# The scores of the attention's first two units in the program ahead of the barrier, and PSUM banks in another order

## What is computed

```python
def compress(kv, w1, w2, pe):          # blocks of 32 rows, stride 16
    pre = lo[:, :-1] + hi[:, 1:] + pe_term[:, None, :]
    return jnp.einsum('bnche,ced->bnchd', jax.nn.gelu(pre), w2)

def nsa_core(q, qpos, gates, cmp_kv, fetch, n_sel, win_kv, win_pos):
    # three branches: compressed, selected, window; each
    s = jnp.einsum('btkgd,bnkd->bkgtn', qg, keys) - slopes * d
    p = masked_softmax(s, mask)        # exp(s - max) / max(sum, 1e-30)
    o = jnp.einsum('bkgtn,bnkd->btkgd', p, values)
    # o = g[0] * o_cmp + g[1] * o_slc + g[2] * o_win
```

## Time and profile before

| | |
|---|---|
| median of 3 runs | 1879.27 us (1876.8 to 1881.36) |
| the profiled execution | 1880.03 us, its span 1878.3 us |
| TensorE busy | 1832.9 us (98%) |
| VectorE, ScalarE, GpSimd busy | 49%, 35%, 33% |
| front, up to its barrier | 0 to 544.8 us |
| clearing of semaphores, second barrier | 544.9 to 546.1 us |
| attention's first TensorE instruction | 546.24 us |
| attention's first transpose of weights | 553.18 us |
| output projection starts | 897.5 us |

### The profile page before, as it was taken

The page is one execution under the profiler, slowest core; times in us unless marked ns, Lnnn a source line. Parts: engine busy times, 40 slices in busy tenths (PEclk is TensorE's granted clock), DMA queues, the critical chain, the costliest instruction groups (busy, mean ns, idle before and its releaser), DMA issues.

```text
span 1878.3 us, 34536 instructions
## 1 busy us (share of the span) xinstructions
PE 1832.9 (98%) x13412; PEld 1715.7 (91%) x13412; DVE 915.4 (49%) x1624; ACT 662.9 (35%) x1247; POOL 615.6 (33%) x620
## 2 busy tenths in 40 slices
PE   8999989999989999999999999999999999999998
PEld 7999989999976666667999999999999999999998
DVE  6799965675547677767423222222221212124525
ACT  5312333344336666667222212121212121214435
POOL 2204962242314443444342222222222222125531
PEclk9999999999989999999999999999999999999999
DMA  4321474363422443441432111111111111113114
GB/s 152 127 68 46 135 203 130 92 167 104 137 89 61 145 136 102 125 136 46 137 123 66 34 46 45 52 39 57 35 57 38 53 40 51 40 45 96 57 34 138
DMA packets 186466, 163.62 MB, mean 87 GB/s; under 512 B 22068, under 2 KB 168176, under 8 KB 185783
## 3 DMA queue, kind: packets, MB, share of 16 engines
q1 hardware_dynamic: 175853, 138.06, 25.0%
q0 software_dynamic: 7840, 21.25, 4.0%
q10 hardware_dynamic: 2610, 2.10, 0.4%
HBM read 147.70 MB, written 18.25 MB: 88 GB/s over the span
## 4 chain that ended last, share of the span: by engine, by line
PE 62%; DVE 4%; ACT 2%; issue 2%; POOL 1%; ACTq 0%; POOLq 0%; DVEq 0%
PE ps L198 26%; PE ps L204 13%; PE ps L2255 5%; PE ps L1726 3%; PE ps L2634 3%; PE ps L1715 3%; PE ps L1738 3%; DVE S L1981 2%; PE ps L1765 2%; PE ps L2644 1%; POOL S L1682 1%; PE ps L2660 1%; ACT S L1865 1%; PE ps L1801 1%; PE ps L1773 1%
## 5 line engine op out<-in xcount | busy, mean ns | idle before, releaser
L184 POOL TENSOR_TENSOR wm_lo<-wm_raw,wm_hi 128x512 fp32r<-128x512 f32 (+1 forms) x96 | 169.6, 1766 | 543.8 <-ACT wm_hi L179 543.8
L2445 DVE TENSOR_TENSOR xT<-ps,xT 128x1056 f32<-128x1056 f32 x64 | 80.5, 1258 | 254.5 <-PE ps L204 254.5
L1682 POOL TENSOR_SCALAR S<-S,inv,gate_p 128x64 f32<-128x64 f32 (+6 forms) x192 | 122.7, 656 | 198.7 <-DVE inv L1991 198.7
L179 ACT ACTIVATE wm_hi<-wm_raw 128x512 fp32r<-128x512 f32 (+1 forms) x96 | 73.9, 770 | 281.7 <-PE ps L204 281.7
L198 PE MATMUL ps<-Ahi,wm_hi 128*128 128x352 f32 x768 | 164.9, 323 | 0.9 <-ACT wm_hi L179 0.9
L198 PE MATMUL ps<-Hhi,wm_hi 128*128 128x352 f32 x768 | 165.2, 323 | 0.0
L198 PE MATMUL ps<-Alo,wm_hi 128*128 128x352 f32 x768 | 164.6, 322 | 0.0
L198 PE MATMUL ps<-Hlo,wm_hi 128*128 128x352 f32 x768 | 164.6, 322 | 0.0
L1118 DVE SCALAR_TENSOR_TENSOR y<-u,conv_w,y 128x1024 f32<-128x1024 f32 x120 | 156.5, 1351 | 1.2
L2426 DVE SCALAR_TENSOR_TENSOR sq<-ps,rstd 128x1056 f32<-128x1056 f32 x32 | 40.2, 1257 | 225.1 <-PE ps L204 225.1
L987 PE MATMUL ps_p<-Xhi,w1hi 128*128 128x256 f32 x544 | 138.6, 292 | 1.4 <-ACT Xhi L706 1.4
(11 more groups left out here) (403 smaller groups left out, 3843.6 us busy)
## 6 DMA issues: line engine op xcount, KB each, us to landing
s_raw<-in_cache_slc_kv_dram SPq DMA_DIRECT2D x256, 128.0 KB, 2.1
raw<-in_cache_cmp_kv_dram SPq DMA_DIRECT2D x132, 128.0 KB, 4.2
wm_raw<-in_w_up_dram SPq DMA_DIRECT2D x32, 512.0 KB, 4.1
wm_raw<-in_w_down_dram SPq DMA_DIRECT2D x64, 256.0 KB, 2.7
raw<-in_cache_cmp_kv_dram POOLq DMA_DIRECT2D x124, 128.0 KB, 4.5
win_raw<-in_w_in_dram SPq DMA_DIRECT2D x38, 256.0 KB, 3.3
wg_raw<-in_w_ple_gate_dram SPq DMA_DIRECT2D x14, 512.0 KB, 3.8
xT<-x_spill SPq DMA_DIRECT2D x2, 2112.0 KB, 10.9
```

The source lines that it names most:

```text
L179: self.c.nc.scalar.activation(self.hi[s][:, 0:nk, :], self.raw[rs][:, 0:nk, :], ACT.Copy).then_inc(self.hi_ready, 1)
L184: self.c.nc.gpsimd.tensor_tensor(self.lo[s][:, 0:nk, :], self.raw[s % self.raw_slots][:, 0:nk, :], self.hi[s][:, 0:nk, :].bitcast(F32), AL ...
L1682: nc.gpsimd.tensor_scalar(x, x, inv[:, n % 3, 3 * e + br:3 * e + br + 1], c.gate_p[:, i, H * br + h:H * br + h + 1], ALU.mult, ALU.mult).t ...
L2445: nc.vector.tensor_tensor(three(x), banks[s][:, :, 0:CH], three(x), ALU.add).then_inc(W.free, 1)
```

## The change

Units 0 and 1 get their scores, row extremes and exponentials in `front`, at the end of the compression, and unit 0 gets its scaling there too. The same instructions are taken out of the attention, whose waits count correspondingly less. The tiles `S0`, `S1`, `mn`, `sums` and `inv` are now made in `front`; `S1` and the scratch tile `t_m` have another place. The order of PSUM tensors in `front` puts the two single banks first. In the order of each engine's list:

- TensorE: unit 0's scores stand ahead of `layer1(NU - 1, 0)`, unit 1's first chunk ahead of `layer1(NU - 1, 1)`, its second chunk ahead of the last `layer2`.
- VectorE: the reductions of the first two chunks stand behind the small steps (`link`) and ahead of `keep(NU - 2)`, then come the sums' maximum and reciprocal for unit 0, the last chunk's reductions and `keep(NU - 1)`.
- ScalarE: unit 0's exponentials stand ahead of the last gelu, unit 1's behind it.
- GpSimd: behind its tables it waits for the reciprocal and scales unit 0's weights.
- In the attention, unit 1's reciprocal and scaling stay in the loop, and unit 0's first transposes wait for no scaling.

```diff
-    with (nc.psum_tensor("ps_p0", [P, NCH, 512], F32) as ps0, nc.psum_tensor("ps_p1", [P, NCH, 512], F32) as ps1,
-          nc.psum_tensor("ps_a", [P, 512], F32) as ps_a, nc.psum_tensor("ps_b", [P, 512], F32) as ps_b, nc.Block() as block):
+    with (nc.psum_tensor("ps_a", [P, 512], F32) as ps_a, nc.psum_tensor("ps_b", [P, 512], F32) as ps_b,
+          nc.psum_tensor("ps_p1", [P, NCH, 512], F32) as ps1, nc.psum_tensor("ps_p0", [P, NCH, 512], F32) as ps0, nc.Block() as block):
...
             pool.wait_ge(tables, 7)
+            pool.wait_ge(first_inv, 1)
+            for br in (1, 2, 0):
+                a0, w = branch_columns(0)[br]
+                for e in range(KVH):
+                    h = G * e
+                    x = c.S[0][:, e, a0:a0 + w]
+                    nc.gpsimd.tensor_scalar(x, x, c.inv[:, 0, 3 * e + br:3 * e + br + 1], c.gate_p[:, 0, H * br + h:H * br + h + 1],
+                                            ALU.mult, ALU.mult).then_inc(first_scaled, 1)
...
+            def first_exps(i, ch):
+                for br in [p[0] for p in chunks_of(i)[ch]]:
+                    a0, w = branch_columns(i)[br]
+                    for e in range(KVH):
+                        at = [p for p in EARLY_ORDER if p[0] == i].index((i, br, e)) + (0 if i == 0 else KVH * 3)
+                        act.wait_ge(first_read, at + 1)
+                        x = c.S[i][:, e, a0:a0 + w]
+                        nc.scalar.activation(x, x, ACT.Exp, bias=c.mn[:, i, e, br, 0:1], scale=-1.0,
+                                             accum_out=c.sums[:, i, 3 * e + br:3 * e + br + 1]).then_inc(first_exp, 1)
+
+            first_exps(0, 0)
             gelu(NU - 1)
+            first_exps(1, 0)
+            first_exps(1, 1)
...
+            def first_scores_of(n):
+                i, ch = EARLY[n]
+                banks = (small, ps_x)[n % 2]
+                if n == 0:
+                    pe.wait_ge(c.q_back, 16)
+                    pe.wait_ge(l2_kept, 1)
+                    pe.wait_ge(ln_centred, NCH)
+                    pe.wait_ge(ln_stat, NCH)
+                elif n == 2:
+                    pe.wait_ge(first_read, KVH * 3)
...
+            first_scores_of(0)
             layer1(NU - 1, 0)
+            first_scores_of(1)
             layer1(NU - 1, 1)
             layer2(NU - 2)
+            first_scores_of(2)
             layer2(NU - 1)
...
+            first_scores_of(0)
+            first_scores_of(1)
             keep(NU - 2)
+            dve.wait_ge(first_exp, 6)
+            V_.tensor_scalar(c.sums[:, 0, :], c.sums[:, 0, :], 1e-30, None, ALU.max).then_inc(first_sums, 1)
+            dve.wait_ge(first_sums, 1)
+            V_.reciprocal(c.inv[:, 0, :], c.sums[:, 0, :]).then_inc(first_inv, 1)
+            first_scores_of(2)
             keep(NU - 1)
...
         for n, (g, i) in enumerate(UNITS):
-            pool.wait_ge(inv_ready, n + 1)
-            for br, e in SCALE_ORDER:
+            if n:
+                pool.wait_ge(inv_ready, n)
+            for br, e in SCALE_ORDER if n else ():
...
-            pe.wait_ge(scaled, 6 * n + max({1: 2, 2: 4, 0: 6}[br] for br, _, _ in blocks))
+            if n:
+                pe.wait_ge(scaled, 6 * n - 6 + max({1: 2, 2: 4, 0: 6}[br] for br, _, _ in blocks))
...
-        for n in range(2):
-            for ch in range(len(CHUNKS[n])):
-                qk(n, ch)
...
-        for n in range(2):
-            for ch in range(len(CHUNKS[n])):
-                exps(n, ch)
...
-        for n in range(2):
-            for ch in range(len(CHUNKS[n])):
-                scores(n, ch)
-        weigh(0)
```

More of the change, by code:

```diff
@@ L342, in front @@
     t_g1, t_g2 = c.at("s_t_g1", [P, P], F32, WRAW_OFF + 2368), c.at("s_t_g2", [P, P], F32, WRAW_OFF + 2880)
-    t_m = c.at("s_t_m", [P, P], F32, WRAW_OFF + 3392)
+    t_m = c.at("s_t_m", [P, P], F32, US_OFF + 1024)
     t_d = c.at("s_t_d", [P, 256], F32, US_OFF)
+    c.S = [c.at(f"S{i}", [P, KVH, width_of(i)], F32, S_OFF + 2 * S_PLACE[i]) for i in range(2)]
+    c.mn = c.at("mn", [P, 3, KVH, 3, 2], F32, STAT_OFF)
+    c.sums = c.at("sums", [P, 3, KVH * 3], F32, STAT_OFF + 160)
+    c.inv = c.at("inv", [P, 3, KVH * 3], F32, STAT_OFF + 256)
     W = Weights(c, "win", WRAW_OFF, split_off=KCS_OFF)
@@ L353, in front @@
     c.n_stored = 0
+    first_qk, first_read, first_exp, first_sums, first_inv, first_scaled = (c.sem("first_qk_done"), c.sem("first_score_read"), c.sem("first_exp_done"),
+                                                                         c.sem("first_sums_kept"), c.sem("first_inv_ready"), c.sem("first_scaled"))
     tables, iotas, cols = c.sem("far_made"), c.sem("table_iotas"), c.sem("table_step")
@@ L1045, in _ @@
                     layer2(n - 2)
+            def first_scores_of(n):
[8 more added lines that the diff above has]
+                    pe.wait_ge(first_read, KVH * 3)
+                off = 0
+                for br, k0, w in chunks_of(i)[ch]:
+                    for e in range(KVH):
+                        rows = slice(DH * e, DH * e + DH)
+                        keys = c.KcP[rows, :] if br == 0 else c.proj[rows, KS if br == 1 else KW, k0:k0 + w]
+                        mm = nc.tensor.matmul(banks[e][:, off:off + w], c.q[rows, 0, P * i:P * i + P], keys, start=True, stop=True)
+                    off += w
+                mm.then_inc(first_qk, 1)
+            first_scores_of(0)
             layer1(NU - 1, 0)
+            first_scores_of(1)
             layer1(NU - 1, 1)
             layer2(NU - 2)
+            first_scores_of(2)
             layer2(NU - 1)
@@ L1329, in _, with first_scores_of @@
             link(V_.scalar_tensor_tensor(out=c.Gm[:], in0=t_g2[:], scalar=tok, in1=t_m[:], op0=ALU.is_equal, op1=ALU.mult))
-            keep(NU - 2)
+            def first_scores_of(n):
+                i, ch = EARLY[n]
+                banks = (small, ps_x)[n % 2]
+                nk = P * (i + 1)
+                dve.wait_ge(first_qk, n + 1)
+                if n == 0:
+                    dve.wait_ge(tables, 7)
+                off = 0
+                for br, _, w in chunks_of(i)[ch]:
+                    a0 = branch_columns(i)[br][0]
+                    tab = c.Tcmp[:, 56 - 8 * i:120 - 8 * i] if br == 0 else c.Tslc[:, T - nk:T] if br == 1 else c.Twin[:, WIN + P - nk:WIN + P]
+                    for e in range(KVH):
+                        V_.tensor_tensor_reduce(c.S[i][:, e, a0:a0 + w], banks[e][:, off:off + w], tab, c.neg_slope[:, G * e:G * e + 1], 1e20,
+                                                ALU.add, ALU.min, c.mn[:, i, e, br, 0:1]).then_inc(first_read, 1)
+                    off += w
+            first_scores_of(0)
+            first_scores_of(1)
+            keep(NU - 2)
+            dve.wait_ge(first_exp, 6)
[3 more added lines that the diff above has]
+            first_scores_of(2)
             keep(NU - 1)
@@ L1462 @@
 ROWS_FREE = B1_OFF + 8192
-S_PLACE = {7: 0, 6: 6912, 5: 13312, 4: 0, 3: 5376, 1: 9728, 0: 13312, 2: 14592}
+S_PLACE = {7: 0, 6: 6912, 5: 13312, 4: 0, 3: 5376, 1: 10880, 0: 13312, 2: 14592}
+EARLY = [(i, ch) for i in range(2) for ch in range(len(chunks_of(i)))]
+EARLY_PIECES = sum(KVH * len(chunks_of(i)[ch]) for i, ch in EARLY)
+EARLY_ORDER = [(i, br, e) for i, ch in EARLY for br, _, _ in chunks_of(i)[ch] for e in range(KVH)]
+EARLY_EXPS = 12
 RAW_PLACE = (AREA + 8192, RAW_OFF, HIY_OFF, HIY_OFF + 8192, AREA)
@@ L1471, in attend @@
     nc, a = c.nc, c.a
-    S = [c.at(f"S{i}", [P, KVH, width_of(i)], F32, S_OFF + 2 * S_PLACE[i]) for i in range(QB)]
+    S = c.S + [c.at(f"S{i}", [P, KVH, width_of(i)], F32, S_OFF + 2 * S_PLACE[i]) for i in range(2, QB)]
     PTs = [c.at(f"PT{s}", [P, 512], F32, PT_OFF + 2048 * s) for s in range(4)]
     c.mixA = c.at("mixA", [P, PAIRS, R], F32, MIX_OFF)
-    mn = c.at("mn", [P, 3, KVH, 3, 2], F32, STAT_OFF)
-    sums = c.at("sums", [P, 3, KVH * 3], F32, STAT_OFF + 160)
-    inv = c.at("inv", [P, 3, KVH * 3], F32, STAT_OFF + 256)
+    mn, sums, inv = c.mn, c.sums, c.inv
     Tslc, Twin, Tcmp, D64, Dn, win_out, Dcmp, Gm = c.Tslc, c.Twin, c.Tcmp, c.D64, c.Dn, c.win_out, c.Dcmp, c.Gm
@@ L1599, in scored @@
     def scored(job, e=None, br=None):
-        return 1 + max(m for m, p in enumerate(PIECES) if p[0] == job and e in (None, p[1]) and br in (None, p[2]))
+        return 1 + max(m for m, p in enumerate(PIECES) if p[0] == job and e in (None, p[1]) and br in (None, p[2])) - EARLY_PIECES
     def exps_of(z):
@@ L1702, in score_banks @@
             if at >= 2:
-                pe.wait_ge(score_read, scored(SCORES[at - 2]))
+                after(pe, score_read, scored(SCORES[at - 2]))
             return 2 * (at % 2)
@@ L1965, in scores @@
             nk, nw = P * (i + 1), P * (min(i, 4) + 1)
-            dve.wait_ge(qk_done, score_no["p", n, ch] + 1)
+            dve.wait_ge(qk_done, score_no["p", n, ch] + 1 - len(EARLY))
             if ch == 0 and n >= 3:
@@ L1986, in weigh @@
             g, i = UNITS[n]
-            dve.wait_ge(exp_done, 6 * n + 6)
```

(7 more changed lines are left out.)

2 lines of the change are left out of this document (1 added, 1 removed).

## The result

The kernel after takes 1888.11 us (median of 14 runs, 1882.28 to 1890.19), the kernel before 1879.35 us in the runs beside it (median of 14, 1876.8 to 1881.47): a ratio of 1.0042, 95% interval 1.0035 to 1.0050. That is 8.8 us slower. The profiled execution took 1888.31 us, 8.28 us more than that of before, with a span of 1886.7 us.

What follows compares the result with a forecast made beforehand. TensorE, busy 98% of the span, was taken as the bound. GpSimd's 549.0 + 10.44 us DRAIN + 1.56 us barrier gave 561.0, +7.8 us: 1880.03 to 1887.8, less 0.8 for the median, 1887.1 us; range 1877.5 to 1889.0.

Steps and rivals of the forecast that it cites:

- The step that decides: GpSimd's closing DRAIN ahead of the barrier: 10.44 us behind the scaling's end at 549.0, ending at 559.4; chance 0.60.
- The sum: Barrier opens at 561.0, 1.56 us behind GpSimd's 559.4; first transpose +7.8 us against 553.18.
- the two ends: Bounds of GpSimd's moved closing DRAIN: 0.05 us if all is settled in the rest, 10.44 us if not.
- The smaller terms: ScalarE done at 551.4, TensorE and VectorE at 548.4, ahead of the barrier; two unhidden table loads, 1.30 us per switch.
- TensorE's level: Behind the longer rest, lower clock perhaps through the next 3 us too: at most 1.3 us more, taken as none.
- Cache loads and second unit's scaling: In the second program: loads start at 561, first needed near 582; second unit's reciprocal found where it was.
- the case's own range: Whole kernel, if the DRAIN costs its 10 us: 1886 to 1889 us around 1887.1.
- The whole range: Whole kernel, covering the DRAIN case and rival 1: 1877.5 to 1889.0 us.
- rival 1: At the barrier, GpSimd's DRAIN is free and ScalarE's 551.4 opens it: -0.2 us, 1879.1 us; chance 0.31.
- Rivals 2 and 3: Rival 2: ScalarE ends up to 2.7 us later, 1881.8 us, 0.04; rival 3: one table or hidden exponentials, 1876.7 us, 0.05.

Runs made afterwards that it cites:

- e5: The kernel after with an early GpSimd DRAIN, then eight 4 KB transfers issued and waited for: 1874.95 us in a single execution, before 1879.12.
- e1: The kernel after with one more GpSimd DRAIN behind its tables, ahead of the wait for the reciprocal: 1880.14 us, ratio 0.9998 to before.
- e6: The kernel after with the moved work one to two units earlier, weights in own buffers, exponentials together: 1873.78 us, ratio 0.9970 to before.
- e7: The kernel before with only the other order of PSUM tensors: 1878.76 us, ratio 1.0001 to before.
- e2: The kernel before, with GpSimd's close held back until the compression's end and nothing moved: 1889.15 us, ratio 1.0048 to before.
- e3: The kernel after with unit 0's six scalings on VectorE instead of GpSimd, ahead of the last `keep`: 1880.59 us, ratio 0.9998 to before.
- e4: The kernel after with all cache page loads on SyncE, GpSimd issuing 32 transfers instead of 156: 1896.08 us, ratio 1.0084 to before.

## Why the prediction was right

**The step that decides held.** GpSimd's scaling was to end at 549.0; it ends at 549.46, 548.98 without the 0.48 us by which this trace is late. The DRAIN was to take 10.44 us behind it and takes 10.47. The barrier was to open 1.56 us ahead of the first transposes: 559.93 to 561.49 is 1.56. The sum said +7.8; the traces say +8.31, +7.83 without the shift. The choice between the two ends, 0.05 and 10.44 us, rested on the 9.7 us of that DRAIN in which nothing was in flight. e5 shows the reading to be right even when the transfers have landed 32.6 us earlier, and e1 that the work is done once.

**The Trainium skill against the row.** "VectorE: DVE Perf Modes", section "The DRAIN you can't avoid", of the Trainium skill has boilerplate DRAINs, those of the runtime's preamble and postamble, at about 12 ns on all five engines. The prediction set this against a DRAIN that closes a block of the kernel itself, of which the section doesn't speak. Here SyncE's take 7 and 13 ns, and GpSimd's 10,440 to 10,561 ns wherever it has 156 transfers behind it and nothing to wait for. The measurement decides for this DRAIN: the 12 ns don't hold for GpSimd behind transfers of its own, and do hold, near enough, for SyncE behind more of them.

**The smaller terms.** ScalarE was to be through at 551.4 and is at 552.04, 551.56 without the shift. TensorE and VectorE were to be through at 548.4; the last `keep` ends at 549.02, 548.54 without it. Both table loads stand where they were expected, 1.28 us each, the next activation 1.30 and 1.29 us behind the load's start; the exponentials' first load is hidden at 537.63, where ScalarE waits anyway.

"ScalarE: Activation LUTs", section "What ACT_TABLE_LOAD costs", of the Trainium skill adds some 1380 ns of drain to each switch. Here 0.02 us stand between a load's end and the next activation, so this case shows the load's 1283 ns and not the rest.

TensorE's level behind the longer rest was taken at nothing, with 1.3 us as its bound: the two 4.2 us windows are busy for 4.12 us each, at the same 0.50, and the 3.1 us behind them have the clock back at 0.96 (before 1.00). Nothing was right: the next transposes come at 568.63 instead of 560.36, +8.27. Cache loads and second unit's scaling, both moved with the second program, gave nothing back and cost nothing: +8.30 at the sampled keys' transposes, +8.33 at the output projection.

**The time.** 1887.1 was forecast, 1888.11 measured. That lies in the case's own range, 1886 to 1889. The whole range, 1877.5 to 1889.0, held rival 1 as well, so the hit of the range says little; the traces' agreement at each step says more. About half of the difference is the shift of 0.48 us. The other half is the step from the profiled execution to the median: 0.8 us was taken off, and after's median lies 0.2 us under its profiled execution. That term wasn't worth its decimal with executions that scatter over several us.

**Rival 1** was what remains without the DRAIN: 0.2 us faster than before. e1 makes its condition true, and measures 0.5 us faster, with an interval from 2.1 us faster to 1.5 us slower. Its account holds too: ScalarE opens the barrier, and what is saved behind it is spent ahead of it. **Rivals 2 and 3** fall: a switch of ScalarE shows 0.02 us and no more ahead of its load and behind it, and both loads are there.

What the prediction didn't see is where a gain would lie. It treated the place of the moved work as given. The trace of before had GpSimd idle for 54 us and TensorE busy without a gap up to the barrier, so work moved earlier still (e6) costs TensorE its own time only and takes the chain of reduction, exponential and scaling out of the way on both sides of the barrier.

What stays open: what GpSimd does in its DRAIN (only its price, and its growth with the number of transfers, are shown), why SyncE's transfers cost nothing there, and how much of e6's 5.3 us beyond the 3.9 is the change's.

## What to carry to other kernels

A block's end is an instruction too: before work is put at the end of an engine's list, read what closes that list, and how long its DRAIN takes, since a price that was hidden moves with it. Here GpSimd pays for the transfers that it has issued at its next DRAIN, and SyncE doesn't: where GpSimd issues many, put a DRAIN where it rests, or let it finish early and give the late work to another engine. And work moved across a barrier gains only if it ends well ahead of the barrier; put right in front of it, it costs there what it saves behind.

## What the runs showed of the hardware that was not expected

- GpSimd's DRAIN costs 63 to 82 ns for each transfer that the engine issued since its last DRAIN: 0.07, 0.73, 2.71 and 10.47 us for 0, 8, 32 and 156. SyncE's takes 7 ns behind 230. Rest doesn't lower it (10.44 us at once, 10.47 behind 56 us of idleness), nor does waiting for the transfers (e5), and a second DRAIN doesn't pay again for the same transfers (e1).
- TensorE's granted clock fell from 0.93 to 0.50 between the window 547 to 549 and the next in e6, with TensorE idle for 1.9 us ahead of the first transposes, and with TensorE busy for 46.8 of the 47 us before 547.
- The same code needs 342.4 us in some executions and 344.3 in others from the attention's first transposes to the output projection (e7 and before, which differ in the PSUM order alone, are such a pair), and the traces differ in TensorE's level. Some 25 us behind the first transposes before's has the lower level for a while and e7's hasn't:

```profile
575.00:585.00 10.00, 8.02 (x52) 5.56 (x52) 6.31 (x18) 3.58 (x9) 3.75 (x6) 0.83 0.01 2
```

```profile
575.00:585.00 10.00, 7.80 (x68) 5.04 (x66) 7.52 (x21) 4.82 (x15) 3.91 (x7) 1.00 0.01 2
```

  All nine traces sort by it. Those of e1, e2, e5 and e7, with 342.4 to 342.6 us, have 1.00 in this window and in the 15 us behind it; before, after, e3, e4 and e6, with 344.2 to 345.6, fall to 0.83 in it or, in after and e4, which are 8 and 17 us later, to 0.89 in 585 to 600. Why the level falls in some executions of the same code isn't shown.
